# Attention: the sums' reciprocals through DRAM, exact key tiles in a mixed order, the first tile's operands split ahead of the barrier

## The reference

```python
visible = (k_pos // 64) <= (q_pos // 64)
score = sum_h relu(iq_h . ik) * iw_h ;  sel = top_k(score, 256 or 264)
logits = q . k / 8 - slope_h * |q_pos - k_pos|        # 8 heads, 2 KV heads
prob = softmax(logits where selected and visible)
o_a = (prob @ v) * silu(z_a)
```

## Time and profile before

| | us |
|---|---|
| median of 3 runs | 2979.24 |
| the profiled execution | 2985.82 |
| its span | 2983.7 |
| TensorE busy | 2781.4 (93%) |
| VectorE busy | 2258.5 (76%) |
| ScalarE busy | 1511.5 (51%) |
| GpSimd busy | 1361.8 (46%) |

### The profile page before, as it was taken

One profiled execution on the slowest core, in us unless ns is written; L12 is line 12 of the kernel. 1 busy time (PEld: TensorE's weight loads), 2 busy tenths in 40 slices (PEclk: granted clock), 3 DMA queues, 4 the chain that ended last, 5 costly groups with the idle time before them and its releaser, 6 DMA issues. The chain is left out here.

```text
span 2983.7 us, 41094 instructions
## 1 busy us (share of the span) xinstructions
PE 2781.4 (93%) x14461; PEld 2545.5 (85%) x14461; DVE 2258.5 (76%) x4116; ACT 1511.5 (51%) x2578; POOL 1361.8 (46%) x950
## 2 busy tenths in 40 slices
PE   6999999899999999999978578999999999999998
PEld 6999999898999999999866457777789998788886
DVE  7477979999999999999445567888886567555554
ACT  4376588676767684867202366777771002111111
POOL 1100489595897978668450155333244333111110
PEclk9999999999999999999999799999999999999999
DMA  4434223242333223223585522211136556121121
GB/s 160 121 124 146 72 91 126 77 136 80 116 105 113 101 74 117 90 73 104 162 237 158 152 60 64 61 52 47 39 105 229 176 163 227 52 66 55 64 69 36
DMA packets 293466, 320.85 MB, mean 108 GB/s; under 512 B 36625, under 2 KB 258321, under 8 KB 292365
## 3 DMA queue, kind: packets, MB, share of 16 engines
q1 hardware_dynamic: 193853, 191.06, 21.2%
q10 hardware_dynamic: 99408, 127.17, 12.3%
HBM read 196.36 MB, written 121.12 MB: 106 GB/s over the span
## 5 line engine op out<-in xcount | busy, mean ns | idle before, releaser
L1428 PE MATMUL psum<-hT_hi,j_whi 128*128 128x416 f32 x2440 | 880.0, 361 | 27.4 <-ACT j_out L1293 18.6
L1428 PE MATMUL psum<-hT_hi,j_wlo 128*128 128x416 f32 x2440 | 863.3, 354 | 0.0
L1428 PE MATMUL psum<-hT_lo,j_whi 128*128 128x416 f32 x2440 | 862.2, 353 | 0.0
L1054 POOL TENSOR_TENSOR v_y<-v_y,v_product 128x422 f32<-128x422 f32 x540 | 667.0, 1276 | 100.7 <-ACT v_product L1036 100.6
L1428 PEld LDWEIGHTS psum<-hT_hi,j_whi 128*128 128x128 f32 x2440 | 464.4, 190 | 42.3 <-ACT j_out L1293 22.8
L1428 PEld LDWEIGHTS psum<-hT_lo,j_whi 128*128 128x128 f32 x2440 | 465.5, 191 | 10.3 <-issue 2.3
L1428 PEld LDWEIGHTS psum<-hT_hi,j_wlo 128*128 128x128 f32 x2440 | 463.5, 190 | 5.9
L1036 ACT ACTIVATE v_product<-v_x,v_taps 128x422 f32<-128x422 f32 x600 | 359.1, 642 | 127.6 <-POOL v_y L1054 95.8
L413 DVE TENSOR_SCALAR_CACHE_REDUCE s_high<-s_key,s_cand 128x512 int16<-128x512 f32 (+13 forms) x240 | 354.5, 1477 | 8.4
L1293 ACT ACTIVATE j_out<-psum 128x416 f32<-128x416 f32 x305 | 154.0, 506 | 337.0 <-PE psum L1428 327.9
L1246 POOL TENSOR_TENSOR j_wlo<-j_w,j_whi 128x1024 fp32r<-128x1024 f32 x61 | 155.7, 2552 | 334.6 <-ACT j_whi L1280 334.4
(11 more groups left out here) (290 smaller groups left out, 5348.0 us busy)
## 6 DMA issues: line engine op xcount, KB each, us to landing
T_dram<-j_out ACTq DMA_DIRECT2D x59, 624.0 KB, 2.9
j_w<-in_w_in ACTq DMA_DIRECT2D x59, 512.0 KB, 3.9
m_gate<-T_dram SPq DMA_DIRECT2D x60, 416.0 KB, 3.5
T_dram<-j_out ACTq DMA_DIRECT2D x59, 416.0 KB, 2.4
m_oraw<-B_dram SPq DMA_DIRECT2D x15, 832.0 KB, 5.4
M_dram<-m_merged ACTq DMA_DIRECT2D x5, 1664.0 KB, 7.4
n_x<-in_x_prompt SPq DMA_DIRECT2D x16, 512.0 KB, 4.7
g_vT<-T_dram SPq DMA_DIRECT2D x32, 256.0 KB, 4.2
```

Of the source, the lines that this page charges most:

```text
L1054: pool.tensor_tensor(y[k % 2][:], y[k % 2][:], product[n % RING][:], ALU.add).then_inc(added, 1)
L1428: last = pe.matmul(bank, w[p][:, k, :], h[:, k, t0:t0 + SPAN], start=(k == 0 and q == 0), stop=(k == KD - 1 and q == 2))
```

## The change

- The scale of the queries is a per-partition factor in ScalarE's evacuation of their projection (L1293); GpSimd's scaling operation goes. GpSimd fills the factors at the kernel's start.
- Ahead of the barrier SP loads only 512 keys, and tile 0's queries and mask, before the last span's store; GpSimd splits 128 keys and these queries there. ScalarE's queue stores the tails and loads the first half of the values. All else is loaded behind the barrier: the remaining keys and values at once, the sample's operands after the first tile's gates.
- Tiles attend to exactly 128 (t + 1) keys, in the order 0, 3, 4, 1, 5, 2, 6, 7, ... 16. The units and exponentials of both groups of tile 0 come first.
- The reciprocals no longer go over TensorE: SP stores them to DRAM, waits, and loads them back to 64 partitions of `factor`. GpSimd's gate waits for that load. Queries and mask of tile i+2 are loaded after tile i's second such round trip (`load_queries`), the gates behind them.
- The key cache is transposed in groups 20 to 23, four tiles each, through a ring slot, with a copy on ScalarE and a subtraction on VectorE. GpSimd's six late splits go to groups 4 to 9, one each. The splits of the remaining keys and values go to groups 0, 1 and 2.
- Buffers are laid out anew accordingly.

```diff
+        for h in range(HEADS):
+            pool.memset(c.scale[(h % 2) * HD:(h % 2 + 1) * HD, h // 2:h // 2 + 1], -(HD ** -0.5) * 2.0 ** (h + 1)).then_inc(scale_made, 1)
+            pool.wait_ge(scale_made, h + 1)
...
+def attended_keys(t):
+    return PAST + DEC if t == DT else P * (t + 1)
...
+            if x == X - 1:
+                first_queries(sp)
...
+    def store_tails(act):
+        act.wait_ge(tail_copied, 2)
+        act.dma_start(c.O["conv_prompt"], tails[:, 0, :]).then_inc(tails_stored, 16)
+        act.dma_start(c.O["conv_sample"], tails[:, 1, :]).then_inc(tails_stored, 16)
+
+    def wait_for_span_stored(eng, x):
+
+        eng.wait_ge(y_stored[x % YS], 16 * (len(range(x % YS, X, YS)) + (x == X - 1)))
...
+    def first_queries(sp):
+        c.wait_for_weights_used(sp)
+        doubled(sp, q_first[:], queries_by_head(c)[:, :, 0:P], q_full)
+        c.wait_for_job(sp, SLOTS - 2)
+        sp.dma_start(nd_first[:], c.ND_dram[0, :, 0:P]).then_inc(c.nd_first_full, 16)
+
+    def split_first(pool):
+
+        c.wait_for_job(pool, SLOTS - 2)
+        pool.wait_ge(c.k_full, 64)
         for g in range(KVH):
-            for u in range(2):
-                sp.dma_start(c.cache[g][:, :, u, :],
-                             c.I["cache_k"].rearrange("(t q g) d -> q t g d", q=P, g=KVH)[:, :, g, :]).then_inc(c.cache_full, 16)
-        c.wait_for_kv(sp)
-        for x in range(2):
-            sp.dma_start(c.vraw[x][:], c.O["v_prompt"].rearrange("(t q g) d -> q t (g d)", q=P, g=KVH)[:, x * HALF:(x + 1) * HALF, :]
-                         ).then_inc(c.v_full, 16)
-        sp.dma_start(c.vsraw[:, 0:NV - 1, :], c.I["cache_v"].rearrange("(t q g) d -> q t (g d)", q=P, g=KVH)).then_inc(c.vs_full, 16)
-        sp.dma_start(c.vsraw[0:DEC, NV - 1, :], c.O["v_sample"].rearrange("(q g) d -> q (g d)", g=KVH)).then_inc(c.vs_full, 16)
-
-    return Operands(keys, values)
+            hi, lo = k_first[g]
+            pool.tensor_tensor(hi[:], kraw[g][:, 0:P], c.zero[:].to_broadcast([P, P]), ALU.add).then_inc(steps, 1)
+            pool.wait_ge(steps, 2 * g + 1)
+            pool.tensor_tensor(lo[:], kraw[g][:, 0:P], f32(hi[:]), ALU.subtract).then_inc(steps, 1)
+            pool.wait_ge(steps, 2 * g + 2)
+        pool.wait_ge(q_full, 32)
+        pool.tensor_tensor(qs[:], q_first[:], c.zero[:].unsqueeze(1).to_broadcast([P, HEADS, P]), ALU.add).then_inc(steps, 1)
+        pool.wait_ge(steps, 2 * KVH + 1)
+        pool.tensor_tensor(qs[HD:P], q_first[HD:P], f32(qs[HD:P]), ALU.subtract).then_inc(steps, 1)
+        pool.wait_ge(steps, 2 * KVH + 2)
+
+    def values(act):
+        c.wait_for_kv(act)
+        c.wait_for_span_stored(act, 3)
+        act.dma_start(c.vraw[0][:], c.O["v_prompt"].rearrange("(t q g) d -> q t (g d)", q=P, g=KVH)[:, 0:HALF, :]).then_inc(c.v_full, 16)
+        c.store_tails(act)
...
+        operands.keys(sp)
+        swish.stores(sp, operands.first_queries)
...
+            if S_Q <= slot < S_K:
+                c.wait_for_scale(act)
+                act.activation(out[:, r, :], c.psum[:, bank_of(j, b), 0:SPAN], ACT.Identity, scale=c.scale[:, slot - S_Q:slot - S_Q + 1]
+                               ).then_inc(bank_read, 1)
...
+ORDER = [0, 3, 4, 1, 5, 2] + list(range(6, TILES))
...
+    def uses(i):
+
+        return i // 2 - (i % 2 == 0)
...
-        group.shares = (u, in_slot[u], ring)
-        in_slot[u], ring = in_slot[u] + 1, ring + 1
+        group.cached = None
+        if group.n in CACHE_GROUPS:
+            u = ring % RING
+            group.cached = (group.n - CACHE_GROUPS[0], u, in_slot[u], ring)
+            in_slot[u], ring = in_slot[u] + 1, ring + 1
...
+    for group in groups[KVH:]:
+        previous, older = groups[group.n - 1], groups[group.n - 2]
+        kept = lambda group: len(group.tiles) - min(4, len(group.tiles) // 2)
+        tiles = len(previous.tiles)
+        window = [(older, x) for x in range(max(0, len(older.tiles) - FREE, kept(older) - 1), len(older.tiles))]
+        window += [(previous, x) for x in range(kept(previous))]
...
+        for group in groups[:KVH]:
+            for unit in group.units:
+                e.unit(group, unit)
+        for group in groups[:KVH]:
+            for h in group.heads:
+                e.head(group, h)
...
+        def load_queries(i):
+            t, p, n = ORDER[i], i % 2, uses(i)
+            if n:
+                sp.wait_ge(q_ready[p], n)
+            doubled(sp, q2[p][:, :, 0:real(t)], queries_by_head(c)[:, :, at(t)], q_full[p])
+            if n:
+                sp.wait_ge(exp_done, HEADS * (i - 1))
+            sp.dma_start(nd[p][:, 0:attended_keys(t)], c.ND_dram[t, :, 0:attended_keys(t)]).then_inc(nd_full[p], 16)
+
+        def load_gates(i):
+            t, p = ORDER[i], i % 2
+            if i >= 2:
+                sp.wait_ge(factor_made, KVH * (i - 1))
+            sp.dma_start(za[p][:, :, 0:real(t)], gates_of(t)).then_inc(za_full[p], 16)
+
+        def share(group):
+
+            g, i = group.g, group.i
+            sp.wait_ge(rs_ready, group.n + 1)
+            if i:
+                sp.wait_ge(factor_full[g], 16 * i)
+            sp.dma_start(RS_dram[g].rearrange("h q -> q h"), rs[:, 4 * g:4 * g + 4], allow_slow_non_contiguous=True).then_inc(rs_stored[g], 16)
+            sp.wait_ge(rs_stored[g], 16 * (i + 1))
+            if i:
+                sp.wait_ge(o_done[(i - 1) % 2], KVH * ((i - 1) // 2) + g + 1)
+            sp.dma_start(factor[g][:], RS_dram[g].rearrange("h q -> (h q)").partition_broadcast(HD)).then_inc(factor_full[g], 16)
+
+        def store(i):
+            p = i % 2
+            sp.wait_ge(o_done[p], (i // 2) * KVH + KVH)
+            sp.dma_start(c.B_dram[0].rearrange("s q t -> (s q) t").rearrange("(h d) t -> d h t", d=HD)[:, :, at(ORDER[i])],
+                         oa[p][:, :, 0:real(ORDER[i])]).then_inc(stored[p], 16)
+
+        load_queries(1)
+        load_queries(2)
+        for g in range(KVH):
+            doubled(sp, krest[g][:], c.T_dram[S_K, g * HD:(g + 1) * HD, FIRST_KEYS:SEQ], rest_full[g])
+        load_gates(0)
+        load_gates(1)
+        sp.dma_start(vraw[1][:], c.O["v_prompt"].rearrange("(t q g) d -> q t (g d)", q=P, g=KVH)[:, HALF:, :]).then_inc(values_full, 16)
+        for i in range(TILES):
+            first, second = groups[KVH * i:KVH * i + KVH]
+            share(first)
+            if i == DT:
+                _, _, u, _, nk, _, _ = last_prompt.tiles[-1]
+                sp.wait_ge(pv_used[u], nk + 1)
+                sp.dma_start(first_rows[1][:], first_weight[:, 2:4]).then_inc(c.m_first_full[1], 16)
+            if i:
+                store(i - 1)
+            share(second)
+            if i + 2 < TILES:
+                if i:
+                    load_queries(i + 2)
+                load_gates(i + 2)
+            if i == 0:
+                for g in range(KVH):
+                    doubled(sp, new_k[g][:], c.T_dram[S_K, g * HD:(g + 1) * HD, SEQ:SEQ + DEC], newk_full)
+                sp.dma_start(vsraw[:, 0:NV - 1, :], c.I["cache_v"].rearrange("(t q g) d -> q t (g d)", q=P, g=KVH)).then_inc(vs_full, 16)
+                sp.dma_start(vsraw[0:DEC, NV - 1, :], c.O["v_sample"].rearrange("(q g) d -> q (g d)", g=KVH)).then_inc(vs_full, 16)
+                for g in range(KVH):
+                    for u in range(2):
+                        sp.dma_start(cache[g][:, :, u, :], c.I["cache_k"].rearrange("(t q g) d -> q t g d", q=P, g=KVH)[:, :, g, :]
+                                     ).then_inc(cache_full, 16)
+            if i == DT - 2:
+                sp.wait_ge(cache_turned, len(CACHE_GROUPS))
+                sp.wait_ge(q_ready[1], uses(DT - 1) + 1)
+                sp.dma_start(c.m_o_raw[0][:], c.m_o_rows(0)).then_inc(c.m_o_full[0], 16)
+            if i == DT - 1:
...
-            pool.tensor_tensor(q2[p][:], q2[p][:], scales, ALU.mult).then_inc(q_scaled[p], 1)
...
+            pool.wait_ge(factor_full[group.g], 16 * (group.i + 1))
...
-        split(0)
...
+        split(2)
         for group in groups:
-            if group.n == 4:
-                for n in range(len(late_splits)):
-                    late_split(n)
-            if group.g == 1 and group.t + 2 < TILES:
-                split(group.t + 2)
+            if group.n in LATE_GROUPS:
+                late_split(group.n - LATE_GROUPS[0])
+            if group.g == 1 and 0 < group.i < TILES - 2:
+                split(group.i + 2)
             if group.n:
                 end(groups[group.n - 1])
...
+    SPLITS_AT = {0: (2, 3), 1: (4, 5), 2: (6, 7)}
+    FIRST_KEYS_SPLIT, FIRST_VALUES_SPLIT, KEYS_SPLIT, VALUES_SPLIT = 1, 3, 5, 7
...
-        def share(group):
-            u, nu, n = group.shares
-            pe.wait_ge(rs_ready, group.n + 1)
+        def turn_cache(group):
+            x, u, nu, n = group.cached
+            g, tiles, _, _ = cached_keys(x)
+            pe.wait_ge(cache_full, 64)
             pe.wait_ge(pt_free[u], nu)
-            for r, h in enumerate(group.heads):
```

(57 more changed lines are left out.)

272 lines of the change are left out of this document (135 added, 137 removed).

## The result

The changed kernel takes 3,086.6 us (median of 4 runs, 3,081.0 to 3,096.9) against 2,974.7 us of the kernel before (4 runs, 2,968.4 to 2,983.2): ratio 1.038, 95% interval 1.034 to 1.042. It is slower by about 112 us; 2,932 was forecast, with 0.05 for slower. The profiled execution has a span of 3,082.5 us, 98.8 more than before.

What follows compares the result with a forecast made beforehand. Late attention groups were taken as bounded by TensorE, early ones by waits. Gains of 32.1 up to group 13 and 15.4 late, 47.5 us, took the profiled 2985.82 to 2938; the median, 6.6 lower, gave 2932 us, range 2908 to 2964.

Steps and rivals of the forecast that it cites:

- Barrier and restart: Start of attention: barrier at about 1686 us, TensorE restarting at 1687.2, 7.5 us earlier than before.
- R(2): Start of group 2's reciprocal, early in attention, forecast at 1711 us.
- c: SP's time per group for storing the reciprocals, waiting and issuing the load: 3.0 us; one tile costs SP 19.8 us.
- R(13): Start of group 13's reciprocal: forecast about 1822 us against 1853.90, 32.1 us gained, including 17.9 us of waits for queries.
- From tile 7 on SP is no longer late: Later attention tiles: a tile lasts over 25 us, so SP's round trips no longer delay the queries.
- The first weight rows have 6 us of slack: Start of the merge: its first weight rows are issued about 3 us later, covered by 6 us of slack.
- Late gain 15.4: Groups 13 to 33: 16.8 us gained by dropping the products, 0.8 a group, less 1.4 us for the cache's transposes.
- D: Rival: barrier not reached earlier because the first queries come late; everything shifts by up to 7.5 us; 2939, chance 0.10.
- C: Rival: in early attention SP is never late and groups close up, so waits of 17.9 us go; 2914, chance 0.16.
- B: Rival: removing the products gives nothing, the late groups pass to VectorE's chain of scores; 2948, chance 0.14.
- A: Rival: SP's round trip for the reciprocals costs 5.8 us; gain 17 us, 2962, chance 0.15.
- E: Rival: slower if the round trip exceeds 7.5 us; at 10.5 us 3015, with waits for queries in groups 4 to 16; chance 0.05.

Runs made afterwards that it cites:

- pe_share: The changed kernel with the reciprocals again sent by four TensorE products and a ScalarE copy a group, no store and load by SP; 2,955.5 us.
- pieces16: The changed kernel with the reciprocals stored as 128 pieces of 16 bytes a group instead of 512 of 4, output not the reference's; 2,965.8 us.

## Why the prediction was wrong, step by step

The miss by D: 47.5 us of gain forecast, 103.1 of loss measured, together 150.6. Its parts add up:

- *Barrier and restart: right within 1.4 us.* The restart was forecast 5.1 us behind the trunk's last store (1687.2, with the store at 1682.1); in after it is 6.5 behind. R(2) gained 19.6 us where 23.6 were forecast: 4.0 lost, 3.7 of it by R(1) already (26.1 us behind the store, 22.4 forecast). The round trips are not its cause, for in pe_share, without any, R(2) comes at 37.8, later than after's 32.9. What is, no run shows. The first wait for a round trip is that of group 3's reciprocal above, 2.9 us.
- *The step that failed: c = 3.0 us, bounds 2.2 and 5.8.* It was 8.6 to 12.0 in groups 2 to 13, from the first tile to the last of the table. The structure was right: SP's tile as 2c + 13.8 gives 19.8 at c = 3.0 and 35 at 10.6, and 36.5 was measured; pieces16, with 3.4 and 4.2 us for its two, gives 21.4 against 21.9 to 22.5. R(2) to R(13) took 211.5 us where 110.8 were forecast: 100.7, the bulk of the miss. Writing the same 2 KB in pieces of 16 bytes, with nothing else changed but the factor's order, brought c down to 2.8 to 4.6 and R(2) to R(13) to 125.1 (pieces16).
- *"From tile 7 on SP is no longer late": wrong at that c.* A tile of 25 to 34 us is shorter than 36.5. R(13) to R(20) took 127.2 us in after, 105.0 in pieces16: 22.2 more. The rest to R(33) took 2.0 more.
- *"The first weight rows have 6 us of slack": wrong at that c, and not the whole of it.* From the last reciprocal to the end after took 14.7 us longer. The first product of the merge came 4.2 us later. TensorE's next wait was 8.1 us longer (12.1 against 4.0), because VectorE splits the rows of `m_row` 15 us later, counted from the reciprocal, and merges behind that; the prediction has no term for these rows. The remaining 2.4 us are not traced.
- *Late gain 15.4: mis-sized.* From R(13) to R(33) before took 371.7 us, pieces16 363.3: 8.4. The products alone are worth 10.6 (pe_share 373.9), 0.53 a group and not 0.8: nothing in groups 13, 14 and 30 to 32, 0.5 to 0.9 between, with R(n) to R(n+1) as group n. The cache's transposes, with whatever else differs there between pe_share and before, cost 2.2 (373.9 less 371.7), not 1.4. The 7.0 less close the sum: 4.0 + 100.7 + 22.2 + 2.0 + 14.7 + 7.0 = 150.6.
- *Rivals.* D is out, the restart came early. C is out: even with the pieces of 16 bytes TensorE waited 23.7 us for the queries (pieces16). B is out: the products are worth 10.6 us. A put c above the forecast's, which was right, but at 5.8 us it was still 3 us or more short and forecast a gain. (Its group 12 would lose 12 + 6.8 less the present 12.6, which is 6.2 and not 5.6; the sum hardly moves.) E named mechanism, place and even 10.5 us as c, and its 3,015 would still have been 72 short: it had R(13) at 1905, where after stands 21.5 later counted from the trunk's end, and it left out the two later places. Its chance was mis-set by the argument "the dearest small DMA of the rows took 5.4": the largest number of the table stood as a bound for an operation that no row shows. With c at 2.8 to 4.6 the change does come out faster (pieces16), but by 0.6%, not by 1.6%: even then the waits between R(2) and R(13) are not 17.9 us, for pe_share, with its products, is 25.7 faster over that stretch.

## What to carry to other kernels

The store to memory in single elements was priced here neither by its bytes nor, in the main, by its count, but by how many pieces share a short stretch of memory. Pieces of 16 bytes, or pieces laid apart, took that price away; try them before thinking about where in the program the store goes. A round trip on a queue that works in order is paid by everything behind it, so multiply it by the queue's turns per tile and compare with the shortest tile, and ask at what price the gain is used up: by rival E's own sum some 7.5 us, within reach of a cost that no row bounded. If no row shows an operation, its dearest neighbour is not an upper bound, and the chance of the slower side has to say so.
